# A decoder layer in fp32 on one core: other orders of work in its first block, around the memory's keys, at attention's input and at the end, and second products that weigh and split two blocks at once

## What is computed

```python
h = rmsnorm(x, mix_norm_w); proj = h @ w_in            # conv B, C, v and HGRN2 q, f, i, g
y_conv = rmsnorm(B * causal_conv3(C * v), conv_norm_w)
y_hgrn = hgrn2_mixer(q, f, i, g, lb, hgrn_norm_w)      # gated linear recurrence, 4 heads
x = x + concat([y_conv, y_hgrn]) @ w_out
x = x + cross_attention(rmsnorm(x), rmsnorm(mem), wq_mem, wkv_mem, wo_mem)   # 256 memory tokens
x = x + peer_ffn(rmsnorm(x), w_query, sub_keys, expert_down, expert_up)
out = rmsnorm(x, final_norm_w)
```

## Time and profile before

| | |
|---|---|
| median of 3 runs | 1588.9 us (1587.73 to 1590.93) |
| profiled execution, its own time | 1593.95 us |
| span of the profile | 1591.9 us |
| PE matmul busy | 1569.8 us (99%) |
| VectorE | 1165.7 us (73%) |
| ScalarE | 666.0 us (42%) |
| GpSimd | 994.0 us (62%) |

### The profile page before, as it was taken

The page is one execution under the profiler, slowest core; times in us unless marked ns, Lnnn a source line. Parts: engine busy times, 40 slices in busy tenths (PEclk is TensorE's granted clock), DMA queues, the critical chain, the costliest instruction groups (busy, mean ns, idle before and its releaser), DMA issues.

```text
span 1591.9 us, 26152 instructions
## 1 busy us (share of the span) xinstructions
PE 1569.8 (99%) x9939; PEld 1485.6 (93%) x9939; DVE 1165.7 (73%) x2254; ACT 666.0 (42%) x996; POOL 994.0 (62%) x562
## 2 busy tenths in 40 slices
PE   8999999999999999999999999999999999999997
PEld 6888888888989999999999999999999999999997
DVE  4155361342479999999999983337999999999994
ACT  5352442542434444444444444333434333333333
POOL 4463376433145799887777778876766766665621
PEclk9999999999999999999999999999999999999999
DMA  5232242323423999988999999969999999999981
GB/s 186 93 101 72 69 157 93 107 65 106 153 86 116 289 351 353 329 290 305 378 413 391 403 415 385 343 237 375 410 410 410 408 401 406 398 401 411 396 336 54
DMA packets 131425, 441.80 MB, mean 278 GB/s; under 512 B 14080, under 2 KB 29440, under 8 KB 123008
## 3 DMA queue, kind: packets, MB, share of 16 engines
q1 hardware_dynamic: 61168, 228.88, 39.6%
q0 software_dynamic: 46080, 167.79, 27.6%
q10 hardware_dynamic: 24080, 43.85, 7.2%
HBM read 396.65 MB, written 43.25 MB: 276 GB/s over the span
## 4 chain that ended last, share of the span: by engine, by line
PE 56%; DVE 1%; DMA 1%; issue 0%; POOL 0%; ACT 0%; ACTq 0%; DVEq 0%
PE psum L1541 17%; PE psum L1543 17%; PE psum L1542 17%; PE psum L1828 4%; DMA kept<-up_in,kept 1%; DVE arena L1209 0%; DVE arena L1282 0%; DVE arena L1342 0%; POOL w_low L462 0%; DVE psum L1205 0%; PE psum L1864 0%; POOL arena L539 0%; PE psum L1858 0%; ACT arena L985 0%; PE psum L1848 0%
## 5 line engine op out<-in xcount | busy, mean ns | idle before, releaser
L462 POOL TENSOR_TENSOR w_low<-kept,w_high 128x1024 fp32r<-128x1024 f32 x212 | 520.1, 2457 | 304.1 <-ACT w_high L592 301.9
L1541 PE MATMUL psum<-hT_high,w_high 128*128 128x352 f32 (+2 forms) x1408 | 484.5, 344 | 3.2 <-POOL w_low L462 3.1
L1542 PE MATMUL psum<-hT_low,w_high 128*128 128x352 f32 (+2 forms) x1408 | 476.7, 339 | 0.0
L1543 PE MATMUL psum<-hT_high,w_low 128*128 128x352 f32 (+2 forms) x1408 | 476.6, 339 | 0.0
L1541 PE MATMUL psum<-wgt_high,up_high 128*128 128x352 f32 x1016 | 328.6, 323 | 1.9 <-DVE wgt_low L1444 1.8
L1543 PE MATMUL psum<-wgt_high,up_low 128*128 128x352 f32 x1016 | 330.2, 325 | 0.0
L1542 PE MATMUL psum<-wgt_low,up_high 128*128 128x352 f32 x1016 | 328.7, 323 | 0.0
L1541 PEld LDWEIGHTS psum<-hT_high,w_high 128*128 128x128 f32 x1408 | 264.7, 188 | 17.4 <-issue 2.9
L592 ACT ACTIVATE w_high<-kept 128x1024 fp32r<-128x1024 f32 x212 | 223.7, 1056 | 134.0 <-PE psum L1543 90.7
L1543 PEld LDWEIGHTS psum<-hT_high,w_low 128*128 128x128 f32 x1408 | 264.8, 188 | 12.7
L1542 PEld LDWEIGHTS psum<-hT_low,w_high 128*128 128x128 f32 x1408 | 265.0, 188 | 12.1 <-issue 0.5
(11 more groups left out here) (273 smaller groups left out, 1967.5 us busy)
## 6 DMA issues: line engine op xcount, KB each, us to landing
kept<-down_in SPq DMA_DIRECT2D x128, 512.0 KB, 6.5
arena<-up_pairs SPq DMA_DIRECT2D x64, 1024.0 KB, 11.0
kept<-front_w SPq DMA_DIRECT2D x92, 512.0 KB, 3.6
gate_dram<-arena ACTq DMA_DIRECT2D x40, 512.0 KB, 10.9
arena<-hid_dram SPq DMA_DIRECT2D x56, 352.0 KB, 14.1
arena<-gate_dram SPq DMA_DIRECT2D x8, 1280.0 KB, 14.8
kept<-gate_dram SPq DMA_DIRECT2D x8, 1280.0 KB, 16.2
hid_dram<-arena ACTq DMA_DIRECT2D x56, 176.0 KB
```

The lines of the kernel that those rows point to most:

```text
L462: nc.gpsimd.tensor_tensor(lower, ring[:, p % RING, :], high.bitcast(F32), ALU.subtract).then_inc(low_ready, 1)
L1541: nc.tensor.matmul(out, lhs[0], rhs[0], start=first, stop=False)
L1542: nc.tensor.matmul(out, lhs[0], rhs[1], start=False, stop=False)
L1543: return nc.tensor.matmul(out, lhs[1], rhs[0], start=False, stop=last)
```

## The change

The change edits six places.

- First block: DVE squares tile 2 of x, ACT scales tile 3, DVE rounds weights 1, weights 2 are rounded right behind, one waking matmul fewer, and PE takes the low half of the weights last.
- Memory's keys: the last key block goes to bank 4, ACT's roundings of weights 36 to 38 stand elsewhere, and the first half of the output product no longer waits for the last key block's copy.
- Attention's input: POOL holds the low half of block 52 until DVE has scaled x, and PE takes the low halves last there as well.
- Second products: DVE weighs and splits two blocks in one instruction, ACT rounds two at once; the kept hidden values lie so that two stand at one distance. One block's row order changes with it.
- POOL's seventh gather of an up row waits for four weighed blocks rather than three, since they come in pairs.
- End: the small addition of squares stands behind the last column block.

```diff
+        def key_bank(b):
+            return 4 if b == KC - 1 else b % 2
...
             for b in range(40, 56):
+                if b == 52:
+                    pool.wait_ge(attn.h, NT + 2)
                 low(b)
...
-            def weight_high(i, s):
-                act.wait_ge(w_raw, i * 2 + 2)
-                nc.scalar.activation(wgt_half[0][:, s, 0:DE], wraw[:, s, 0:DE], ACT.Copy).then_inc(w_high, 1)
+            def weights_high(i, s):
+                act.wait_ge(w_raw, i * 2 + 4)
+                nc.scalar.activation(wgt_half[0][:, s:s + 2, 0:DE], wraw[:, s:s + 2, 0:DE], ACT.Copy).then_inc(w_high, 1)
...
-            norm_tiles(mixn, ld_x, [16] * NT)
+            for t in (0, 1, 3):
+                act.wait_ge(ld_x[t], 16)
+                square(mixn, t)
+                if t == 1:
+                    root(mixn, 0, 2)
+            act.wait_ge(mix_square, 1)
+            root(mixn, 2, 2)
+            act.wait_ge(mixn.root, 2)
+            nc.scalar.activation(hn[:, NT - 1, :], x[:, NT - 1, :], ACT.Copy, scale=rs[:, mixn.col + 3:mixn.col + 4])\
+                .then_inc(mix_last, 1)
             high(0)
-            high(1)
             act.wait_ge(ld_vec, 16)
             norm_high(mixn)
+            act.wait_ge(high_ready, 2)
+            high(2)
...
-            for b in range(32, 36):
-                ahead(b)
-                act.wait_ge(conv_y, CC + b - 31)
-                nc.scalar.activation(hT_half[0][:, b - 32, :], pB[:, b - 32, :], ACT.Copy).then_inc(y_high, 1)
+            for c, weights in enumerate(((32,), (33,), (34, 35), (36,))):
+                for b in weights:
+                    ahead(b)
+                act.wait_ge(conv_y, CC + c + 1)
+                nc.scalar.activation(hT_half[0][:, c, :], pB[:, c, :], ACT.Copy).then_inc(y_high, 1)
             values_out(0, 2)
...
-            norm_rows(mixn)
+            dve.wait_ge(ld_x[2], 16)
+            nc.vector.tensor_tensor_reduce(hn[:, 2, :], x[:, 2, :], x[:, 2, :], 1.0, 0.0, ALU.mult, ALU.add,
+                                           ss[:, mixn.col + 2:mixn.col + 3]).then_inc(mix_square, 1)
+            for t in range(NT - 1):
+                dve.wait_ge(mixn.root, t // 2 + 1)
+                nc.vector.tensor_scalar(hn[:, t, :], x[:, t, :], rs[:, mixn.col + t:mixn.col + t + 1], None, ALU.mult)\
+                    .then_inc(mixn.h, 1)
+            dve.wait_ge(wt[1], 16)
+            dve.wait_ge(high_ready, 1)
+            nc.vector.tensor_copy(w_half(1)[0], ring[:, 1, :]).then_inc(high_ready, 1)
...
-            for s in range(KEEP - 1):
-                low_up(s, s % RING_U)
-                weigh(s + 1, SPILL + s + 4, SPILL + s + 1, hid_kept[s + 1])
-                weight_low(s, s % 4)
-                if s == 0:
+            weigh(0, SPILL)
+            for u in range(0, NK, 2):
+                low_up(u, u % RING_U)
+                if u == 0:
+                    weights_low(u)
+                if u + 2 < NK:
+                    weigh(u + 2, u + 2 + SPILL if u + 2 < KEEP else u + 2 - KEEP)
+                if u == 0:
                     dve.wait_ge(gel3_ready, 1)
                     step(nc.vector.tensor_tensor(w3, gel3, gate3, ALU.mult))
                 else:
-                    sparse_ups(s)
+                    if u < NK - 2:
+                        sparse_ups(u)
+                    weights_low(u)
+                low_up(u + 1, (u + 1) % RING_U)
+                if u < NK - 2:
+                    sparse_ups(u + 1)
...
-                if o == KC - 1:
-                    dve.wait_ge(fin_squares, 1)
-                    step(nc.vector.tensor_tensor(ms[:, 0:DT], ss[:, 0:DT], ss[:, NT:NT + DT], ALU.add))
...
+            dve.wait_ge(fin_squares, 1)
+            step(nc.vector.tensor_tensor(ms[:, 0:DT], ss[:, 0:DT], ss[:, NT:NT + DT], ALU.add))
             dve.wait_ge(fin_squares, 2)
...
-                pe.wait_ge(low_ready, b + 1)
+                pe.wait_ge(high_ready, b + 1)
                 for k in range(KC):
+                    pe.wait_ge(u.high, k + 1)
+                    product(high, 0, k, first=k == 0)
                     pe.wait_ge(u.ready, k + 1)
+                    product(high, 1, k)
+                    if k < 4:
                         turn_chunk(u, k + 4)
+                    else:
+                        if k == 4:
+                            pe.wait_ge(low_ready, b + 1)
+                        product(low, 0, k - 4)
+                for k in range(4, KC):
+                    ins = product(low, 0, k, last=k == KC - 1)
+                ins.then_inc(block_used, 1)
...
-            pe.wait_ge(k_out, KC)
+            pe.wait_ge(k_out, KC - 1)
             pe.wait_ge(v_out, MT)
-            product(hT_half, MIX_BLOCKS, product_done, ((y_ready, KC), (y_ready, KC)), range(NT))
+            product(hT_half, MIX_BLOCKS, product_done, ((y_ready, KC), (k_out, KC)), range(NT))
```

More of the change, by code:

```diff
@@ L678, in keys_out @@
             def keys_out(block, b):
[L679 removed]
+                if b != 4:
+                    ahead(block)
                 act.wait_ge(block_used, block + 1)
[L681 removed]
+                nc.scalar.activation(KT[:, b, :], psum[:, key_bank(b), 0:NM], ACT.Copy).then_inc(k_out, 1)
             def values_out(hf, bank):
@@ L1529, in turn_tiles @@
                             ins.then_inc(u.tr, 1)
-                pe.wait_ge(u.h, u.tiles + 2 if u is attn else u.tiles)
+                if u is not mixn:
+                    pe.wait_ge(u.h, u.tiles + 2 if u is attn else u.tiles)
             def turn(u):
@@ L1609, in keys @@
                     pe.wait_ge(k_out, b - 1)
-                columns(block, memT_half, NM, b % 2)
+                if b == KC - 1:
+                    pe.wait_ge(y_ready, HH)
+                columns(block, memT_half, NM, key_bank(b))
             def values(b0, bank):
```

93 lines of the change are left out of this document (46 added, 47 removed).

## The result

The changed kernel takes 1598.12 us as the median of 6 runs (1595.35 to 1604.48), the one before 1588.76 (6 runs, 1587.73 to 1590.93). The ratio is 1.0052, with a 95% interval from 1.0034 to 1.0070. A second measurement, beside the last experiments, gives 1600.04 against 1589.67, 1.0061 (1.0046 to 1.0077). The forecast was 1590.7, with 1593.7 as its upper end.

The account below looks back on a forecast made before the run. TensorE was taken to bound the kernel, so only its gaps could change: 0.8 + 0.3 - 0.3 + 1.7 - 0.7 = +1.8 us on 1588.9 gave 1590.7 us. The range ran from 1585.2 less 0.7 up to 1593.7.

Parts of the forecast that it names:

- Term 4: Start of the second products: TensorE waits 2.8 us for low weights at product 4 and its clock falls; net +1.7 us.
- Term 1: First block: GpSimd goes first and delays VectorE's copy of weights 1, the gap ahead of block 2 goes; net +0.8 us.
- the rival that the clock falls too: First block: TensorE's idle 2.7 us also lowers its clock, +1.7 us, giving 1592.4 us; chance 0.19.
- Term 2: Memory's keys: GpSimd slows VectorE's tail, the wait moves from block 37 to 38; +0.3 us, bounds -2.2 and +0.6.
- Terms 3 and 5: Attention's input: a high-half matmul goes into the wait, -0.3 us. End: the last column block goes first, -0.7 us.
- The lower bounds of terms 2 and 3: Memory's keys -2.2 us, both gaps gone; attention's input -0.5 us. The range took 0.7 us off for them.
- the third rival: Second products: early rows land in time, gaps at products 4 and 8 vanish, -3.8 us there, 1585.2 us; chance 0.23.
- a second fall in term 4: Start of the second products, upper bound: the clock falls a second time, +3.4 us instead of +1.7; chance 0.03.

Follow-up runs that it names:

- GpSimd held at the keys: The memory's keys' part alone in the kernel before, with GpSimd waiting for the last conv output ahead of low half 37: 1590.93 against 1591.14 us, ratio 1.0001.
- the loads early: Stored hidden values' loads issued one pair of blocks earlier; ratio to the kernel before 1.0009 with the second products' part alone, 1.0021 in the changed kernel.

## Why the prediction was wrong, step by step

**Term 4, the start of the second products: the step that failed.** The forecast followed the low weights and the gathered rows, and costed the move of the weighing at nothing: "a pair of low halves takes 0.89 us instead of 1.04 ... worth nothing by itself". For the some 120 products behind it has one sentence, "Afterwards DVE gains on PE as before". It didn't ask what else the moved instruction waits for. Weighing block u + 2 in the step of block u asks for its hidden values one product (3.87 us) earlier, while the queue still issues their load at the same product's end. Before, that wait came once in 480 us, for 1.5 us, which is the row that should have warned: the load was already only just in time. After, it comes eleven times, and where a load of gates stands ahead of the pair it takes 19.6 us against the 19.8 and 15.5 that there are. That is 4.3 us in the profiled execution, and by the ratios 0.3% alone and 0.5 to 0.6% in the whole (1.0052 and 1.0061 against 1.0002 without the part).
(The Trainium skill, "DMA: Bandwidth & Descriptors", section Queues, rings and completion order, says that on each DMA engine a queue's descriptors are consumed in the order of its ring. The trace fits: the load behind 1280 KB of gates took 19.6 us, where the median of these loads was 12.2 us.)

What the term did treat: PE waits for low weights at product 4 in each of the seven traces that have this part with its low halves behind the gathered rows, so that wait was rightly seen, but for 0.8 to 2.1 us and not 2.8, and the clock stayed up behind it each time. In the profiled execution row 4 let DVE start at 1097.88, which is 1094.6 on the scale of before (1093.77 there), and PE was itself 2.3 us late: a wait of 2.03 us stood ahead of the last first product, since the gates' load was there only at 1073.25 (14.48 us waited) and ACT's paired rounding stood behind it, the last block's rounding behind that. Product 8 waited 0.54 us, and nothing of the loss of before (1.84 and the clock) came again. The sum is +0.7 against +1.7. That nearness is luck: the second trace has no wait ahead of the last first product, and there the same stretch comes to -2.1.

The base of the term was thin too. The wait of 1.84 us at product 8, with the clock down behind it, was taken for a property of the kernel before. In the nine traces whose second products keep the order of before, PE waits there (at product 8 or 9) from less than 0.2 us (GpSimd held at the keys) to 2.65 us (attention's input and the end alone), and the clock falls behind it in three of nine. So up to some 3.5 us come or go with the execution at this place, whatever the change.

**Term 1, first block.** The copy's end (15.35, measured 15.34) and the second matmul (16.1, measured 16.05) were right, and so was +0.8 without the clock (0.7). What failed is the weight of the rival that the clock falls too: it had 0.19 and came in five of six traces, with 2.1 to 2.4 us against the 2.5 that the rival gives. The argument from the gap of 1.33 us at 292.97, behind which the clock stayed, was drawn from a much shorter gap: here PE sat idle for 2.51.

**Term 2, keys.** The mechanism was right (GpSimd locks DVE's tail, the key copy is late, the wait goes to block 38), the size not: the copy ended at 230.3, less the 2.2 us of the first block 228.1, as worked out, but the clock fell behind the wait. Some 15 matmuls stand 0.21 us apart there instead of 0.12, which is 1.4 us. Not all of it is the clock's price: POOL had the low half of weights 39 at 233.75 (231.36 + 2.39), 231.5 on the scale of before, where 231.6 was forecast, and with the clock up block 39 would have waited for it until then. Block 39 and the output product would then have come at 233.75 and 236.6, some 0.25 us behind before on its own scale. So the forecast's +0.3 holds, and the clock added 1.1.

**Terms 3 and 5** were near: -0.3 as forecast, and -0.5 for -0.7. At the end the small addition now stands between the last square and the last sum and takes its 0.2 us there.

**The range.** Its ends don't follow from the bounds that the terms give. The lower bounds of terms 2 and 3 lie 2.5 and 0.2 us under their forecasts, not 0.7 together, which puts the third rival's low end at 1582.5, and the clock falling in block 0 together with a second fall in term 4 makes 1590.7 + 1.7 + 1.7 = 1594.1. The measured 1598.12 lies outside of both.

**What stays open.** The parts alone add up to 1.0024, the whole is 1.0052 or 1.0061; without the first block's part the whole is 1.0026. The clock in the first block explains 1.6 us of it (0.1%). The granted clock over all executions says about the same: its mean is 0.9976 before, 0.9972, 0.9971, 0.9968 and 0.9978 with the four parts alone (first block, keys, second products, the rest), which adds up to 0.0015 less, and 0.9952 in both measurements of the whole, 0.0024 less. The difference of 0.0009 is 1.4 us, an estimate from these means. The rest, 3 to 4 us, is about as large as the summed uncertainty of four ratios, and no run shows a way from the first block to the second products. Also open is why, with the loads early, PE still waits 1.42 us at product 30, and whether the paired order makes the faster of the two paces described at the end rarer: of the nine traces with single blocks four have it for most of the second products, of the nine with pairs one, and no run was made to tell.

## What to carry to other kernels

An instruction that is moved forward asks for everything it waits for earlier: list all its waits, find for each when its load is issued, and compare the time that is left with the longest landing behind the largest neighbour in the queue, not with the median. A load that was waited for once is a load without slack. And a gap on PE is priced twice, without and with a fall of the clock behind it. In the 18 traces here the clock fell behind 17 of the 25 waits of 1.8 us and more that PE had from the first block on, and behind none of the 32 waits of 1.0 to 1.6 us; a fall cost up to 1.7 us. Last, one profiled execution isn't the kernel: a wait that a forecast builds on has to be seen in more than one.

## What the runs showed of the hardware

**The clock isn't a function of the gap.** Behind the same gap of 2.98 us (2.5 idle) at the same place it stayed up once and fell five times, and behind 1.9 us at the keys it fell in all six traces. It stayed up behind the longest wait of all, 3.07 us at product 28 in the whole without the first block's part; the row, then the window behind it:

```profile
1193.79 0.40 PE L1554 MATMUL psum<-wgt_high,up_high 128*128 128x352 f32 x1 [3.07 <-DVE wgt_low L1458]
```

```profile
1194.00:1198.00 4.00, 4.00 (x26) 4.00 (x26) 4.00 (x6) 1.70 (x3) 3.35 (x2) 1.00 1.02 413
```

(The Trainium skill, "TensorE: Matmul & The Clock Gate", section What's actually happening, says that the number of slow matmuls varies from run to run of one kernel. The six traces, of five kernels with the same code at this place, fit: in one of them no matmul is slow there, in the others some are.)

**Matmuls of the same kind run at one of two paces.** From 1300 to 1500 us, with PE busy all the time and its clock at 1.00, these are the kernel before and the one with the first block's part alone:

```profile
1300.00:1500.00 200.00, 200.00 (x1244) 200.00 (x1243) 191.96 (x279) 75.98 (x104) 131.12 (x68) 1.00 1.02 402
```

```profile
1300.00:1500.00 200.00, 200.00 (x1252) 200.00 (x1251) 191.78 (x277) 77.33 (x105) 132.13 (x69) 1.00 1.02 407
```

Eight matmuls more in 200 us: 0.160 us each against 0.161. A pace mostly holds for dozens of products, 3.84 us a product or 3.867. It often changes right behind a stall, but not only: with GpSimd held at the keys, PE falls back from 3.84 to 3.867 at product 32 with no stall in sight. What chooses the pace isn't shown. Over the 118 products from the tenth on it makes 3.1 us between these two traces, as much as most parts of this change are worth. It may be one reason why the times of one kernel spread over several us, and why a single trace's span doesn't rank two kernels; the places within a trace tell more, as far as they come again in a second one.
